# Sparse attention: the reciprocal softmax sums reach 64 lanes through DRAM, on ScalarE's queue, in place of TensorE products

## The reference, cut to what matters

```python
logits = jnp.einsum('bthd,btkd->bhtk', qb, k_sel).astype(jnp.float32) * scale
logits = logits - slopes[None, :, None, None] * dist[:, None]
logits = jnp.where(valid[:, None], logits, -jnp.inf)
p = jax.nn.softmax(logits, axis=-1)
return jnp.einsum('bhtk,btkd->bthd', p.astype(v.dtype), v_sel)
```

## Time and profile before

| | before |
|---|---|
| runs, median of 3 | 1448.45 us (1447.98 to 1451.27) |
| the profiled execution | 1446.68 us, of which span 1445.0 us |
| granted TensorE clock, mean | 0.977 |
| PE busy | 1341.7 us (93%) |
| part B of the attention | about 498 to 675 us of the span |

### The profile page before, as it was taken

One profiled execution on the slowest core, in us unless ns is written; L12 is line 12 of the kernel. 1 busy time (PEld: TensorE's weight loads), 2 busy tenths in 40 slices (PEclk: granted clock), 3 DMA queues, 4 the chain that ended last, 5 costly groups with the idle time before them and its releaser, 6 DMA issues.

```text
span 1445.0 us, 18548 instructions
## 1 busy us (share of the span) xinstructions
PE 1341.7 (93%) x6181; PEld 1071.6 (74%) x6181; DVE 1023.3 (71%) x1468; ACT 684.6 (47%) x1157; POOL 727.8 (50%) x628
## 2 busy tenths in 40 slices
PE   2899999997899999989998899999999999999997
PEld 2668888785566666657876778888888888887886
DVE  4678699987877655554775986666666666378787
ACT  5456677736676655554125633223323334354332
POOL 3135444556677866652002165555555556578552
PEclk9899899998999999998999999999999999999999
DMA  9521234457534343312753244444444435989432
GB/s 326 178 62 30 88 126 135 144 162 203 131 76 114 88 125 116 89 43 84 272 172 114 88 152 155 167 168 167 168 158 146 146 141 197 362 296 327 150 109 117
DMA packets 123562, 220.20 MB, mean 152 GB/s; under 512 B 9386, under 2 KB 52500, under 8 KB 123220
## 3 DMA queue, kind: packets, MB, share of 16 engines
q1 hardware_dynamic: 123476, 219.12, 45.7%
HBM read 160.90 MB, written 57.93 MB: 151 GB/s over the span
## 4 chain that ended last, share of the span: by engine, by line
PE 41%; DVE 7%; issue 2%; DMA 1%; ACT 1%; POOL 0%; DVEq 0%; POOLq 0%; ACTq 0%
PE ps_out L2339 25%; PE ps_out L2365 12%; PE ps_out L1694 1%; DVE mod_acc_final L1759 1%; PE ps_out L1678 1%; DMA scr_mod_final<-mod_acc_final 1%; DVE y_full L1780 1%; DVE wgu_lo L2446 0%; PE ps_out L1702 0%; ACT square_junk L2257 0%; DVE x L2601 0%; DVE y_gated L1792 0%; DVE down_part L2599 0%; DVE h_sum_t L2413 0%; DVE h_t_full L2413 0%
## 5 line engine op out<-in xcount | busy, mean ns | idle before, releaser
L2036 POOL TENSOR_TENSOR wgu_lo<-wgu_raw,wgu_hi 128x512 fp32r<-128x512 f32 x66 | 97.4, 1483 | 127.6 <-ACT wgu_hi L2028 127.6
L2273 POOL TENSOR_TENSOR dn_lo<-dn_raw,dn_hi 128x512 fp32r<-128x512 f32 x77 | 126.9, 1665 | 67.1 <-ACT dn_hi L2179 67.0
L2028 ACT ACTIVATE wgu_hi<-wgu_sum 128x512 fp32r<-128x512 f32 x88 | 55.2, 632 | 199.7 <-DVE wgu_sum L2429 80.0
L2339 PE MATMUL ps_out<-h_b_t_hi,wgu_hi 128*128 128x512 f32 x352 | 138.1, 392 | 6.6 <-DVE h_b_t_lo L2417 2.6
L483 POOL TENSOR_TENSOR win_lo<-win_raw,win_hi 128x256 fp32r<-128x256 f32 (+1 forms) x84 | 66.7, 824 | 141.0 <-ACT win_hi L473 115.7
L2339 PE MATMUL ps_out<-h_b_t_hi,wgu_lo 128*128 128x512 f32 x352 | 137.7, 391 | 0.0
L2339 PE MATMUL ps_out<-h_b_t_lo,wgu_hi 128*128 128x512 f32 x352 | 137.5, 391 | 0.0
L2179 ACT ACTIVATE dn_hi<-dn_raw 128x1024 fp32r<-128x1024 f32 x77 | 81.2, 1062 | 114.4 <-PE ps_out L2365 55.7
L2365 PE MATMUL ps_out<-dn_hi 128*128 128x512 f32 x308 | 120.2, 390 | 0.0
L2365 PE MATMUL ps_out<-dn_hi,dn_lo 128*128 128x512 f32 x308 | 119.8, 389 | 0.0
L2365 PE MATMUL ps_out<-dn_lo,dn_hi 128*128 128x512 f32 x308 | 119.8, 389 | 0.0
(11 more groups left out here) (356 smaller groups left out, 3648.9 us busy)
## 6 DMA issues: line engine op xcount, KB each, us to landing
scr_act_sums<-act_sums SPq DMA_DIRECT2D x11, 1792.0 KB, 6.7
dn_raw<-scr_act_sums SPq DMA_DIRECT2D x77, 256.0 KB, 5.3
wmod_c<-in_w_mod_dram SPq DMA_DIRECT2D x48, 256.0 KB, 2.9
wgu_raw<-in_w_gate_dram SPq DMA_DIRECT2D x11, 1024.0 KB, 5.3
wgu_raw<-in_w_up_dram SPq DMA_DIRECT2D x11, 1024.0 KB, 5.4
wd_sums<-in_w_down_dram SPq DMA_DIRECT2D x11, 1024.0 KB, 4.8
scr_wd_sums<-wd_sums SPq DMA_DIRECT2D x11, 1024.0 KB, 4.1
dn_raw<-scr_wd_sums SPq DMA_DIRECT2D x44, 256.0 KB, 7.0
```

The costliest lines, as they stand in the source:

```text
L2036: pool.tensor_tensor(sl[slot(m, x)][:], src, sh[slot(m, x)][:].bitcast(F32), ALU.subtract).then_inc(wlp, 1)
L2273: pool.tensor_tensor(bl[q % NSLOT][:, 1], braw[entry(q)][:, 1], bh[q % NSLOT][:, 1].bitcast(F32), ALU.subtract).then_inc(dlw, 1)
L2339: last = pe.matmul(bank(m, b), a[s][:, t], h[x][t // 2][:, t % 2], start=(fresh and t == 0 and a is sh and h is hh), stop=(t == 3 and a is ...
```

## The change

The four products on PE and the copy on ACT are gone. In their place ACT issues two transfers per group, 16 groups in all. In the steps y = 2 and y = 6, after the exponential, it waits for the reciprocals and stores them to a row of a new DRAM tensor; the elements of the 128x4 block are written so that the row holds 512 queries in order. In the steps y = 3 and y = 7, after the copies of units, it waits until that store has landed, and loads the row, repeated on 64 lanes, into `spr`. DVE's product waits for the load in place of ACT's copy. The planner has no spread to place.

```diff
@@ attention, extra
-        return v, [("s", gr) for gr in range(SBG, 2 * SBG) if end.get(gr, -99) == r]
+        return v, []
@@ scalar
+            d = (r - SBR - 6) // 4
+            if r >= SBR + 6 and r % 4 == 2 and d < SBG:
+                act.wait_ge(rc, d + 1)
+                act.dma_start(rsum[d].rearrange("(b p) -> p b", p=P), rs[:, 4 * d:4 * d + 4],
+                              allow_slow_non_contiguous=True).then_inc(rso, 16)
...
-            for gr in spread(r):
-                d = gr - SBG
-                lanes = slice(HD * (gr // 2 % 2), HD * (gr // 2 % 2) + HD)
-                act.wait_ge(sd, d + 1)
+            d = (r - SBR - 7) // 4
+            if r >= SBR + 7 and r % 4 == 3 and d < SBG:
+                lanes = slice(HD * (d // 2 % 2), HD * (d // 2 % 2) + HD)
+                act.wait_ge(rso, 16 * (d + 1))
                 if d >= 4:
-                    act.wait_ge(od, gr - 3)
-                act.activation(spr[lanes, upper(gr)], place(("s", gr))[lanes], ACT.Copy).then_inc(sc, 1)
+                    act.wait_ge(od, SBG + d - 3)
+                act.dma_start(spr[lanes, upper(d)], rsum[d:d + 1, :].partition_broadcast(HD)).then_inc(rsl[d % 2], 16)
@@ vector
-                    dve.wait_ge(sc, gr - SBG + 1)
+                    dve.wait_ge(rsl[gr % 2], 16 * ((gr - SBG) // 2 + 1))
@@ tensor
-            for gr in spread(r):
-                d = gr - SBG
-                await_freed(follows["s", gr])
-                pe.wait_ge(rc, d + 1)
-                for b in range(4):
-                    last = pe.matmul(place(("s", gr))[:, P * b:P * b + P],
-                                     rs[:, 4 * d + b:4 * d + b + 1].to_broadcast([P, P]), g.ident[:],
-                                     start=True, stop=True)
-                last.then_inc(sd, 1)
```

More of the change, by code:

```diff
@@ L990, in attention_plan, with attention @@
     return rows, units, of_step, end, done_by, bank, follows, row_follows
-def attention(nc, k, g, A, scr, p1, base):
+def attention(nc, k, g, A, scr, rsum, p1, base):
     NZ, LEAD, VSTEP = 3, 5, 3
@@ L1068, in attention @@
     rc = k.sem("d_rsum_ready")
-    sd = k.sem("rsum_spread_done")
-    sc = k.sem("rsum_spread_copied")
+    rso = k.sem("rsum_stored")
+    rsl = k.sems("rsum_spread_loaded", 2)
     oll = k.sem("oT_lo_last_ready")
@@ L1098, in ended @@
         return [gr for gr in end if end[gr] + steps == r]
-    def spread(r):
-        return [gr for gr in end if gr >= SBG and end[gr] == r]
     def paired(r, steps):
@@ L1385, in await_freed @@
                 pe.wait_ge(v_rdy, n + 1)
-            elif kind == "s":
-                pe.wait_ge(sc, n - SBG + 1)
             else:
@@ L2700, in emit @@
         scr = nc.dram_tensor("scr_qkv", [16, 2, P, SEQ], F32, kind="Internal").ap()
+        rsum = nc.dram_tensor("scr_rsum", [2 * NH, HALF], F32, kind="Internal").ap()
         modf = nc.dram_tensor("scr_mod_final", [P, 2 * D], F32, kind="Internal").ap()
@@ L2759, in emit @@
                 assert base + 68 * 1024 <= nc.sbuf_top
-                pa = attention(nc, k, g, A, scr, p1, base)
+                pa = attention(nc, k, g, A, scr, rsum, p1, base)
                 with nc.Block() as block:
```

## The result

The changed kernel takes 1507.07 us (median of 5 runs, 1503.9 to 1522.97) against 1448.45 us (1446.93 to 1451.27) for the kernel before on the same chip: a ratio of 1.0438, with an interval of 1.041 to 1.0465. It is 58.6 us slower, where 20.6 us less was forecast.

A forecast was written before the change was run, and what follows sets the result against it. PE, busy 93% of the span, was taken to set the pace. Gains of 1.73 + 12.5 + 1.5 + 2.04 + 0.46 + 1.05 + 1.3 = 20.6 us took the median from 1448.45 to 1427.9 us, range 1424.5 to 1438.5.

The forecast's parts named there:

- the heavy half: Heavier part of a head in part B: without the spread 11.68 us in place of 13.72, -2.04 each.
- the light half: Lighter part of a head: next transposes may start at 5.90 us, not 6.79, -0.89 at most; with the stall 6.3, -0.46.
- the whole without a stall: The sum of gains with ACT's wait for the store covered: 23.2 us less, 1425.3 us for the kernel.
- 2.9 + L: Us into a light half when PE can go on, L being store issue to landing; covered at L = 3.0.
- Rivals A: Store lands early or stall is covered, L up to 3.0: 23.2 us gained, 1425.3; chance 0.55 together with the forecast.
- B: Store late, L of 3.9 to 5.5, light halves lose: 10.8 us gained at L = 4.7, 1437.6; chance 0.30.
- D: The spread was cover and something else on PE's path fills the gap, so nothing changes; chance 0.05.
- L itself: Time from the store's issue on ACT to its landing: 3.4 us taken, 4.7 as bound from above.
- rival C: ACT's wait for the store in step y = 3 becomes the pace: slower, 1460 us at L = 8; chance 0.07.
- Other queues: SP's queue keeps its transfers, sharing DMA engines busy 30%; ACT's 32 issues of about 0.5 us free except at the wait.
- it costs nothing, but has little left: Load in a light half: there at 7.8 us into the head, against about 8 for DVE's product.
- both transfers have several us: In a heavy half, store and load have several us of room, so no stall was counted there.

## Why the prediction was wrong

**What PE loses and gains: right.** Its own steps for the heavy half (11.68 us; 11.90 measured without transfers), the light half (5.90; 5.74) and the whole without a stall (23.2 us; 22.5) held. So did the position of the store, 1.44 us into the light half (1.47), and the formula by which PE goes on at 2.9 + L: with the L of 9.2 of the head shown that is 12.1, and it is 12.19. The issues on ACT cost 0.38 and 0.45 us, less than the 0.53 taken. Rivals A, B and D are out: neither landed the store early enough, nor did it stay under 5.5, nor did nothing happen.

**The step that failed is "L itself".** It put 3.4 us on the store and 4.7 as the bound from above; it measured 9.1. The bound multiplied 32 pieces per engine by the kernel's mean time of a packet, on top of 2.0 us, and so took for granted that a landing is a fixed time and the time of the packets, which goes by number and size. No row of before had several pieces that go into the same 64 bytes, so its rows bounded another quantity. The sentence "no piece can be smaller and the mean packet has 1.8 KB" leaned the wrong way: size was not what counted. With the pieces spread out, the same count lands after 2.3 us, below what was taken.

The store's packets are not what takes long. The last store goes out at 731.80, and the load that waits for it at 739.77, 8.0 us later; the stretches in between (columns as above):

```profile
731.80:734.00 2.20, 0.14 (x2) 0.00 (x0) 0.25 (x1) 0.49 (x1) 0.00 (x0) 1.00 0.44 61
734.00:740.00 6.00, 5.28 (x21) 3.54 (x21) 0.87 (x2) 0.00 (x0) 0.00 (x0) 1.00 0.00 0
```

From 734 on no DMA engine has a packet of any queue, and the store still takes 5.8 us to land. The trace records its 4-byte packets with a median of 9 ns each, and those of the run with pieces 64 bytes apart with the same 9 ns. Nor can SP's traffic be the reason for this store, since there is none from 734 on.

The rule of the Trainium skill about one descriptor for each element ("DMA: Bandwidth & Descriptors", Rules for kernel authors) fits the packet counts here: the queue has 9728 packets with 4-byte pieces and 3584 with 16-byte ones, 16 x 384 fewer. Yet the count was not the cost. What the Trainium skill says for rival C ("Perfetto Trace Analysis", DMA Instruction — HWDGE: a semaphore only when the write is confirmed, surprisingly late for HBM) points the right way: the landing at 739.77 with the last packet before 734. But here it is late by the layout, and not for DRAM as such, where the stores in 16-byte pieces land after 2.3 and 2.9 us (medians). My sentence that "the trace does not bear it out", because stores of 512 KB land after 2.8, weighed large pieces against small ones.

**"Other queues" failed as well.** It said that SP's queue keeps its transfers and shares engines that are busy 30%. The share of the engines was not the measure: in 576 to 580 they are 79% occupied and move 18 GB/s, SP's weight loads land after 7.1 us, and the query loads after 10.1 where ACT does not wait. POOL "has no part in a head's cycle" was wrong too as soon as POOL is late: `o_dT_lo` is behind its products and ahead of DVE's next `o_full`. The store alone cost 29 us, and PE's waits for `o_full` there are 19.3 us. The same goes for "it costs nothing, but has little left" of the load: it lands after 4.2 us and DVE waits for it five times, 14.8 us.

**Rival C was the right mechanism and too cheap.** By its formula L = 9.1 gives 23.2 - 7 x 6.1 = -19.5, a kernel of some 1468 us; it took 1507. The formula left out three things. The heavy halves: "both transfers have several us", but from the store at 571.79 PE had work until 583.08 - 3.54 = 579.54, and PE goes on only 1.84 us behind the store's landing (581.24 to 583.08), after three operations of ACT, so that the cover is 5.9 us. The transfers of others, just told. And the clock. The waits and the clock are seen in the groups by line for 498 to 745 us (busy us, mean ns, idle before), first without transfers, then in the changed kernel:

```profile
L1474 PE MATMUL ps_o<-aT,vd 128*128 128x512 f32 (+1 forms) x192 | 73.8, 494 | 3.4 <-DVE o_full L1354 2.2 <-DVE aT L1340 0.8
...
L1456 PE MATMUL ps_at<-ident,a_rows 128*128 128x128 f32 x145 | 24.6, 279 | 6.0 <-ACT aT L1239 4.9 <-DVE aT L1340 1.0
```

```profile
L1487 PE MATMUL ps_o<-aT,vd 128*128 128x512 f32 (+1 forms) x192 | 84.7, 555 | 6.5 <-DVE o_full L1367 4.5 <-ACT aT L1244 0.8 <-DVE aT L1352 0.6
...
L1469 PE MATMUL ps_at<-ident,a_rows 128*128 128x128 f32 x147 | 31.5, 335 | 64.8 <-ACT a_rows L1215 43.4 <-ACT aT L1244 21.3
```

The spans of these two executions differ by 1521.2 - 1426.1 = 95.1 us. Waiting in these two groups grew from 9.4 to 71.3 us, 61.9 more. The same products in them took 17.8 us longer, and the logits and the transposes into `ps_z` 13.5 in the same way: 31.3 us for work that is not more but runs at a lower clock. Together 93 of 95. A wait on PE was paid here half again in slow products.

The three parts are not cleanly additive. By differences of medians, ACT's wait for the store is worth 1507.07 - 1477.03 = 30 us, and the stores alone 1454.77 - 1425.5 = 29. The other 22 come where the load, itself held up, is added, or from waits that only appear together; no run takes these apart. Up to L = 3.7 the prediction's formula is not contradicted: there it gives 23.2 - 7 x 0.7 = 18.3, some 1430, and 1428.12 was measured, but the single runs at 2.3 and 2.5 have 1430.44 and 1429.43, so they are too few to show a slope. At L = 5.0 it gives 1439, and it was 1450: there the other costs have set in.

Three figures of the prediction do not follow as written, without weight for the outcome: 0.3 us for 32 pieces makes L = 3.1 only on top of the 2.8 of the 512 KB stores (2.3 on the 2.0 that it starts from), head 0's own rows give 6.11 + 11.68 = 17.8 us a head and not 17.6, and 670.72 - 0.89 + 0.39 is 670.2.

## What to carry to other kernels

A column that goes to DRAM as a row should not leave as 4-byte pieces that lie side by side: turn it into rows, or store a lane's values side by side and reorder where they are read, or leave gaps (16 bytes from piece to piece brought 9.1 us down to 3.7 here, 32 to 2.5). Look at the landing time of the first such store, not at its bytes, and at the landing times of all the other transfers in its time. A bound from a mean over packets bounds nothing for a pattern that those packets do not have; where the nearest row differs in kind, the far rival deserves more than 7 in 100. And where PE waits several us at a time, add the products that follow at half the clock to the price of the wait.

## What the runs showed of the hardware that was not expected

- A store of 4-byte pieces to DRAM lands the later the denser they lie: after 9.1, 5.0, 3.7, 2.5 and 2.3 us for 16, 8, 4, 2 and 1 of them to 64 bytes, some 0.4 us for each further one; 128 crowded pieces (7.9 us) are slower than 512 spread ones (2.3 us). Four times 16 bytes to 64 bytes landed after 2.3 to 2.9 us.
- The wait comes behind the packets: with no packet of any queue from 734 us on, the last store landed at 739.77.
- While such a store of 2 KB is under way, other transfers land late: 256 KB weight loads on SP's queue after 7.1 in place of 2.9 us, a 128 KB load on the store's own queue after 8.6 in place of 3.0.
- After a PE wait of 3.5 us its granted clock was 0.57 for four us (583 to 587), after one of 7.6 us 0.50 for the next three (569 to 572).
- A float32 product of 64x512 on DVE took 1068 ns with one operand read in steps of 16 bytes, 0.69 us without; a turn of 128x32 in 32x32 blocks took 211 ns.
